# Issuing the second half of every expert weight tile from ScalarE's own queue

## The reference, cut to what matters

```
def moe_swiglu(h, w_router, w_gate, w_up, w_down):
    shape = h.shape
    t = h.reshape(-1, shape[-1])
    logits = (t @ w_router).astype(jnp.float32)
    top_logits, top_idx = lax.top_k(logits, TOP_K_EXPERTS)
    gates = jax.nn.softmax(top_logits, axis=-1)
    combine = jnp.sum(jax.nn.one_hot(top_idx, N_EXPERTS, dtype=jnp.float32) * gates[..., None], axis=1)
    out = jnp.zeros_like(t)
    for e in range(N_EXPERTS):
        out = out + combine[:, e:e + 1].astype(t.dtype) * swiglu(t, w_gate[e], w_up[e], w_down[e])
    return out.reshape(shape)
```

## Time and profile before

| | |
|---|---|
| median of 3 runs | 1441.28 us (1438.74 to 1442.69) |
| profiled execution, its own time | 1441.36 us |
| span of its profile | 1439.7 us |
| mean granted TensorE clock | 0.998 |
| PE busy | 1403.3 us, 97% |
| PEld (weight loads) busy | 893.0 us, 62% |
| DVE, ACT, POOL busy | 33%, 21%, 8% |
| read from HBM | 442.86 MB |

### The profile page before, as it was taken

The page is one execution under the profiler, slowest core; times in us unless marked ns, Lnnn a source line. Parts: engine busy times, 40 slices in busy tenths (PEclk is TensorE's granted clock), DMA queues, the critical chain, the costliest instruction groups (busy, mean ns, idle before and its releaser), DMA issues.

```text
span 1439.7 us, 34819 instructions
## 1 busy us (share of the span) xinstructions
PE 1403.3 (97%) x15324; PEld 893.0 (62%) x15324; DVE 468.5 (33%) x932; ACT 299.1 (21%) x570; POOL 122.3 (8%) x158
## 2 busy tenths in 40 slices
PE   8999999999999999999999999999999999899898
PEld 6987789999997973564564353353354345344345
DVE  5698666666445840021021021021021002101102
ACT  5544564444445550000000000000000000000000
POOL 3644000000000024001000000000000000000100
PEclk9999999999999999999999999999999999999999
DMA  7561994255554349999999999999999999999995
GB/s 252 214 239 61 386 331 163 88 191 199 196 185 158 117 171 343 386 408 391 404 405 392 405 403 399 399 389 400 398 396 408 391 386 409 390 392 408 394 393 234
DMA packets 149997, 456.23 MB, mean 317 GB/s; under 512 B 12677, under 2 KB 15803, under 8 KB 149851
## 3 DMA queue, kind: packets, MB, share of 16 engines
q1 hardware_dynamic: 142448, 439.61, 79.5%
q0 software_dynamic: 3888, 11.31, 2.9%
q10 hardware_dynamic: 3514, 3.08, 0.7%
HBM read 442.86 MB, written 11.11 MB: 315 GB/s over the span
## 4 chain that ended last, share of the span: by engine, by line
PE 48%; SPq 43%; DMA 4%; issue 3%; DVE 1%; ACT 1%; DVEq 0%; ACTq 0%
SPq L741 30%; PE bank L2010 26%; SPq L748 12%; PE bank L2539 9%; PE bank L2554 6%; DMA ring<-in_moe_w_down 3%; PE bank L2215 1%; DMA ring<-in_attn_w_in 1%; PE bank L2227 1%; PE bank L2189 1%; PE bank L2308 0%; SPq L687 0%; PE bank L2249 0%; PE bank L2172 0%; PE bank L2270 0%
## 5 line engine op out<-in xcount | busy, mean ns | idle before, releaser
L2539 PE MATMUL bank<-ring,xg 128*32 128x512 f32 (+1 forms) x6144 | 587.0, 539 | 10.4 <-DMA ring<-in_moe_w_up 7.3
L2539 PEld LDWEIGHTS bank<-ring,xg 128*32 128x32 f32 x6144 | 220.4, 110 | 360.7 <-issue 294.6
L2554 PE MATMUL bank<-ring,heT 128*32 128x256 f32 x5280 | 293.0, 381 | 13.6 <-DMA ring<-in_moe_w_down 13.5
L2554 PEld LDWEIGHTS bank<-ring,heT 128*32 128x32 f32 x5280 | 194.8, 111 | 117.5 <-DMA ring<-in_moe_w_down 16.8
L1895 DVE TENSOR_TENSOR he<-he,bank 128x256 f32<-128x256 f32 (+1 forms) x96 | 31.6, 383 | 492.5 <-ACT he L1341 472.6
L1341 ACT ACTIVATE he<-bank 128x256 f32<-128x256 f32 (+1 forms) x93 | 26.6, 357 | 774.9 <-PE bank L2539 774.9
L2010 PE MATMUL bank<-hL_r,wd 128*128 128x288 f32 x480 | 142.7, 297 | 0.0
L1413 DVE TENSOR_TENSOR ring_r<-ring,wd 128x1024 fp32r<-128x1024 f32 x90 | 110.0, 1225 | 69.6 <-ACT wd L997 67.8
L997 ACT ACTIVATE wd<-ring 128x1024 fp32r<-128x1024 f32 x90 | 95.1, 1059 | 133.9 <-PE bank L2010 133.9
L2010 PE MATMUL bank<-hU,wd 128*128 128x288 f32 x352 | 103.9, 295 | 0.0
L2010 PE MATMUL bank<-hU,ring_r 128*128 128x288 f32 x352 | 103.0, 293 | 0.0
(11 more groups left out here) (440 smaller groups left out, 1325.5 us busy)
## 6 DMA issues: line engine op xcount, KB each, us to landing
ring<-in_moe_w_gate SPq DMA_DIRECT2D x112, 1024.0 KB, 14.5
ring<-in_moe_w_up SPq DMA_DIRECT2D x112, 1024.0 KB, 19.8
ring<-in_moe_w_down SPq DMA_DIRECT2D x112, 1024.0 KB, 13.7
ring<-in_attn_w_in SPq DMA_DIRECT2D x6, 2048.0 KB, 13.0
ring<-in_ffn_w_gate SPq DMA_DIRECT2D x5, 2048.0 KB, 16.2
ring<-in_ffn_w_up SPq DMA_DIRECT2D x5, 2048.0 KB, 9.1
ring<-in_cache_k SPq DMA_DIRECT2D x16, 512.0 KB, 8.4
ring<-in_cache_v SPq DMA_DIRECT2D x16, 512.0 KB
```

Source lines behind the costliest of these rows:

```text
L2539: last = mm(out, xg[:, k, GRP * r:GRP * r + GRP], w[:, :, j, :, q, :], start=(k == 0), stop=(k == KD - 1), skip_group_check=True)
L2554: last = mm(sums_of(r)[GRP * q:GRP * q + GRP, :], left, w[:, j, 256 * cols_:256 * cols_ + 256], start=first, stop=(c == NCH - 1 and j == C ...
```

## The change

ACT issues the second half (`part` 1) of the expert tiles from tile 11 on (`NPRO + RING`), through its own DMA queue; SP issues the first halves, and both halves of tiles 0 to 10. For this ACT walks along the tiles of an item: at each tile t it waits until PE has used the tile, issues the second half of the tile that is 7 later in the ring, and, where t is the last tile of a gated chunk, goes on to the `silu` of this chunk. The same semaphores are counted up, and the same bytes move to the same places.

```diff
+    def half_of_tile(e, g, kind, c, h, part):
+
+        place = ring[expert_slot(g)][:, SLOT // 2 * part:SLOT // 2 * part + SLOT // 2]
+        if kind == GATED:
+            wide = WIDE[c]
+            k = SLOT // 2 // wide
+            src = a[("moe_w_gate", "moe_w_up")[part]][0][bass.ds(e, 1), P * k * h:P * k * h + P * k, FROM[c]:FROM[c] + wide]
+        else:
+            k = CH // 2 // P
+            pairs = a["moe_w_down"][0].rearrange("e (c f) d -> (e c) f d", f=CH // 2)
+            src = pairs[bass.ds(e * (2 * DFE // CH) + ((FROM[c] // CH + h) * 2 + part), 1), :, :]
+        return place.rearrange("p (k f) -> p k f", k=k), src.rearrange("o (k p) f -> p (o k) f", p=P)
...
         for g, (kind, c, h) in enumerate(PRO_TILES + BODY_TILES):
             if g < RING:
                 sp.wait_ge(*stream[N0 + g - RING][1])
             else:
                 sp.wait_ge(q_used, U0 + (g - RING + 1))
-            expert_tile(c // NCH, g, kind, c % NCH, h)
+            for part in range(2 if g < NPRO + RING else 1):
+                sp.dma_start(*half_of_tile(c // NCH, g, kind, c % NCH, h, part)).then_inc(w_in[expert_slot(g)], 16)
...
                 sp.wait_ge(q_used, i * PER_ITEM + (U0 + g - RING + 1))
-                expert_tile((i + c // NCH) % E, g, kind, c % NCH, h)
+                sp.dma_start(*half_of_tile((i + c // NCH) % E, g, kind, c % NCH, h, 0)).then_inc(w_in[expert_slot(g)], 16)
...
-        def act_body(i, last):
-            for c in range(1, NCH):
+        def second_half(i, t, last):
+
+            n = t + RING
+            if n >= (len(LAST_TILES) if last else PER_ITEM + RING):
+                return
+            act.wait_ge(q_used, i * PER_ITEM + (U0 + NPRO + t + 1))
+            kind, c, h = BODY_TILES[n % PER_ITEM] if not last else LAST_TILES[n]
+            e = (i + (n // PER_ITEM + c // NCH)) % E
+            act.dma_start(*half_of_tile(e, NPRO + n, kind, c % NCH, h, 1)).then_inc(w_in[expert_slot(NPRO + n)], 16)
+
+        def act_body(i, tiles):
+            last = tiles is LAST_TILES
+            for t, (kind, c, h) in enumerate(tiles):
+                second_half(i, t, last)
+                if kind != GATED or h != tiles_in(kind, c) - 1:
+                    continue
                 if c == 2 and last:
                     act.wait_ge(pg_full, 1)
                     copy(pickT[0:SL, 0:NP], banks[5][0:SL, 0:NP])
...
-            silu(i, NCH)
             act.wait_ge(*after(i, DOWN, NCH - 1))
...
         with act.Fori(0, last_item) as i:
-            act_body(i, False)
-        act_body(last_item, True)
+            act_body(i, BODY_TILES)
+        act_body(last_item, LAST_TILES)
```

More of the change, by code:

```diff
@@ L731, in _ @@
                 sp.dma_start(tile_cols(s, CH), cols(w_go, CH * name[1], CH)).then_inc(got, 16)
[L733 to L749, removed]
         for g, (kind, c, h) in enumerate(PRO_TILES + BODY_TILES):
```

## The result

The changed kernel takes 1450.94 us (median of 4 runs, 1448.87 to 1452.68) against 1440.44 us (now 4 runs as well): a ratio of 1.0069 (95% interval 1.005 to 1.0088), some 10 us slower. The prediction said 1441 us and no change. Its profiled execution, the fastest of the four, took 1448.87 us, 7.5 more than that of before.

What follows compares the result with a forecast made beforehand. The prediction took the DMA engines' rate to bound the expert stage, with PE close behind. All terms were 0 us, so 1441.4 + 0 = 1441.4, predicted as 1441 us; range 1421 to 1457, no change at chance 0.48.

Steps and rivals of the forecast that it cites:

- What bounds the kernel: Expert stage, 774 to 1363 us: time is bytes over the DMA engines' rate; perfect supply could give back 20 to 24 us.
- Step 1: SP gives up 157 of its 336 issues, freeing 58 us beside full DMA engines: 0 us on the path.
- step 3: ACT takes 157 issues, 58 to 99 us unblocked, no load; if blocked, 2.3 us each was taken.
- Step 4: Silu, eviction and pickT copy behind blocked ACT issues: taken as 0 us; pickT's cover 10.4 us, a stall 1 to 2 us.
- Step 2: Bytes, packets and semaphore counts stay; the DMA engines' work stays 45.1 MB an item: 0 us.
- Step 5: Queue depth doubles from about 5 to 10 halves; engines are never empty, so more in flight gives nothing: 0 us.
- Step 7: Tiles 0 to 10, and all before 532 us, are as before.
- Rival A: Two queues drive the DMA engines faster in the expert stage: -15 us, 1426 us, at the end 1417; chance 0.27.
- Rival B: ACT's blocked issue delays silu of chunk 2 and eviction: +32 us, 1473 us, or 1457 at one place; chance 0.11.
- Rival C: Two streams of weight loads disturb each other, lowering the rate 1 to 2%: 1447 to 1453 us; chance 0.14.

Runs made afterwards that it cites:

- the walk alone: Changed kernel with ACT making all its new waits on used tiles but issuing nothing, SP issuing both halves; against the kernel before: 0.9992.
- my own edit: At most 3 tiles in flight, added to the kernel with ACT from tile 7 and to the changed kernel: 1.0066 and 1.0072 of the kernel before.
- level queues: Changed kernel altered so neither DMA queue starts behind the other, as with ACT issuing second halves from tile 7 instead of 11: 1.0013 of the kernel before.
- two halves moved: Changed kernel with ACT also issuing the first halves of tiles 11 and 12: 1.0013 of the kernel before.

## Why the prediction was wrong

- **What bounds the kernel** was read rightly: the DMA engines, at 398 to 399 GB/s before and after. That SP's long issue instructions are a full queue and no lack of issue time was right: freed of half of them, SP waited 544 us in all for PE to use tiles, and nothing got faster.
- **Step 1** (SP freed, nothing gained) came out as said. Of **step 3** (ACT loaded) the unblocked figure held, 0.47 us an issue with none blocked, and not the 2.3 us that it took; its price of nothing was right, with the walk alone at 0.9992. **Step 4** was right for the change, and the copy of pickT, whose cover it gave as the thinnest, is where a late ACT cost 6.3 us in my own edit, against the 1 to 2 us that it allowed.
- **Step 2 is the one that failed**: "The DMA engines' work stays 45.1 MB an item: 0 us", which rests on "the time is the bytes over the rate". The bytes and the rate did stay, and the last tile is whole at the same time (1425.4 and 1425.8 us). But PE doesn't consume bytes, it consumes whole tiles, and a tile is whole when the slower of two queues has delivered. I asked whether each queue would be empty or full and never where each would stand. **Step 5** repeated it: more in flight "gives nothing" leaves out that bytes in flight ahead in one queue are taken from the other, and that with more in flight the parts of a tile drift further apart. The missing term was SP's backlog at the hand-over, 3.3 MB / 398 GB/s = 8.4 us.
- **Step 7** ("tiles 0 to 10 are as before") passed over the very point: those tiles' second halves, still in SP's queue, are the backlog.
- **Rival A** (two queues are faster) is refuted: 399 GB/s. The stretch 555 to 565 us, which I gave as its support, has 419 in the changed kernel too, and the rest of the stage has not. **Rival B** did not occur in the change. **Rival C** gave 1447 to 1453 us, which holds the measured time, by the wrong mechanism: the streams don't lower the rate.
- **Open:** 1.3 thousandths, 1.9 us, are left with level queues, with ACT from tile 7 and with two halves moved alike. It isn't ACT's waits. The likeliest cause is drift: late in the stage 900 packets beyond a whole tile have been moved, where the kernel before has 489. The difference is 1.7 MB or, as an estimate, 4.2 us, which is over the 1.9 us measured, and no run changes drift alone. So the cause is argued and not shown.
- No version here is faster than the kernel before clear of noise.

## What to carry to other kernels

If two queues each bring a part of every tile, the consumer goes at the pace of the one behind, and an initial distance costs its bytes over the rate once: open both queues level, or bound how far either may run ahead. Beside saturated DMA engines, check not only bytes and rate but whether each byte that moves completes something that is needed next. And an in-order engine that takes over issues should do its short work for others first, above all the copy with the shortest cover.

## What the runs showed of the hardware

- Two hardware queues with packets of 4 KB and 2 KB got equal numbers of packets (512 and 505 in 8 us), not equal bytes (1.98 and 1.00 MB).
- The DMA share stays at 1.02 to 1.03 from 774 to 1341 us in kernels that differ by 10 us: it says that the engines are busy, not that what they bring is what is waited for.
- The increments of one tile land further apart the longer the stream runs and the more is in flight: 15.8 us late in the stage with 6 tiles in flight on two queues, 10.7 in the kernel before, 7.8 with 3 tiles and 4.9 with 2.
- At the end of the stream the rate stands at half for a while. With level queues and 6 tiles in flight (window rows as above):

```profile
1410.00:1415.00 5.00, 5.00 (x100) 3.03 (x96) 1.10 (x3) 0.00 (x0) 0.00 (x0) 1.00 0.92 361
1415.00:1420.00 5.00, 5.00 (x100) 3.03 (x96) 0.00 (x0) 0.00 (x0) 0.00 (x0) 1.00 0.51 207
1420.00:1425.00 5.00, 5.00 (x100) 3.02 (x96) 1.29 (x6) 0.61 (x3) 0.00 (x0) 1.00 0.51 201
1425.00:1430.00 5.00, 5.00 (x100) 3.01 (x96) 0.00 (x0) 0.00 (x0) 0.00 (x0) 1.00 0.17 69
```

A share of 0.51 at 201 to 207 GB/s looks like half of the engines having finished ahead of the rest. The increments of the last tile agree: 16 of the 32 land from 1413.6 to 1415.1 us, the other 16 from 1423.8 to 1429.3. In the kernel before the share falls under 0.6 only at 1419 us. Which engines, and why, the traces don't say.
